# Routing of a mixture-of-experts layer: two experts chosen by eight-largest and replace steps, GpSimd makes half of a split's second parts, a bias row arrives by DMA

## What is computed

```python
mod = jax.nn.silu(c) @ w_ada[l] + b_ada[l]             # 6 x 1024 numbers
sh1, sc1, ga1, sh2, sc2, ga2 = jnp.split(mod, N_MOD, axis=-1)
... # attention and convolution branches, x = x + ga1 * (merged @ w_o)
h2 = modulate(rms_norm(x, g_norm2[l]), sh2, sc2)
# hierarchical_moe: 4 groups of 8 experts
g_logits = xt @ w_rg + b_rg;  g_prob = softmax(g_logits);  g_idx = argmax(g_logits)
g_w = g_prob[g_idx]
e_logits = (xt @ w_re + b_re)[the 8 of group g_idx]
e_val, e_loc = lax.top_k(e_logits, 2)
e_w = softmax(e_val) * g_w                              # weights of the two experts
# each chosen expert: silu(x w1) * (x w3) @ w2 on the tokens that chose it; x = x + ga2 * sum
```

## Time and profile before

| what | us |
|---|---|
| median of 3 runs | 1148.68 |
| range of the runs | 1147.99 to 1148.87 |
| profiled execution, own time | 1147.94 |
| its span, first to last instruction | 1146.1 |
| PE busy in the span | 1116.1 (97%) |
| DVE / ACT / POOL busy | 483.6 / 414.6 / 184.3 |

### The profile page before, as it was taken

The page is one execution under the profiler, slowest core; times in us unless marked ns, Lnnn a source line. Parts: engine busy times, 40 slices in busy tenths (PEclk is TensorE's granted clock), DMA queues, the critical chain, the costliest instruction groups (busy, mean ns, idle before and its releaser), DMA issues.

```text
span 1146.1 us, 15442 instructions
## 1 busy us (share of the span) xinstructions
PE 1116.1 (97%) x5860; PEld 752.1 (66%) x5860; DVE 483.6 (42%) x966; ACT 414.6 (36%) x616; POOL 184.3 (16%) x79
## 2 busy tenths in 40 slices
PE   5899999999999999999999998999999999999998
PEld 3689777874444444444444445978878888888876
DVE  4686344662222222222222214789574653233136
ACT  4543553331111111111111115675464454444234
POOL 0303233000000000000000002100314064342522
PEclk9999999999999999999999999999999999999999
DMA  9968668789999999999999996452434366455451
GB/s 354 381 223 296 215 245 313 285 347 418 421 424 423 422 422 424 423 424 423 423 422 423 424 423 254 148 200 99 143 121 160 124 207 207 150 180 211 158 183 37
DMA packets 96830, 331.75 MB, mean 289 GB/s; under 512 B 8529, under 2 KB 31298, under 8 KB 71170
## 3 DMA queue, kind: packets, MB, share of 16 engines
q1 hardware_dynamic: 96496, 330.58, 74.4%
q0 software_dynamic: 80, 0.26, 0.1%
q10 hardware_dynamic: 194, 0.06, 0.0%
HBM read 329.84 MB, written 1.05 MB: 289 GB/s over the span
## 4 chain that ended last, share of the span: by engine, by line
PE 89%; DMA 4%; DVE 3%; ACT 2%; SPq 2%; issue 1%; DVEq 0%; ACTq 0%
PE ps L1273 19%; PE ps L904 15%; PE ps L905 14%; PE ps L906 14%; PE ps L1313 9%; DMA ring<-in_w_in 4%; PE ps L1250 3%; PE ps L1251 2%; PE ps L1328 1%; PE ps L979 1%; SPq L773 1%; PE ps L1329 1%; DVE ring_r L2110 1%; PE ps L1436 1%; ACT ring_r L1648 1%
## 5 line engine op out<-in xcount | busy, mean ns | idle before, releaser
L866 POOL TENSOR_TENSOR ring_r<-ring,ring_r 128x1024 fp32r<-128x1024 f32 x66 | 172.0, 2627 | 840.4 <-ACT ring_r L1648 840.3
L905 PE MATMUL ps<-ring_r,hl_r 128*128 128x512 f32 x528 | 209.1, 396 | 0.0
L904 PE MATMUL ps<-ring_r,hl_r 128*128 128x512 f32 x480 | 195.2, 407 | 5.6 <-DVE hr_r L2202 4.3
L906 PE MATMUL ps<-ring_r,hr_r 128*128 128x512 f32 x480 | 190.2, 396 | 0.0
L1648 ACT ACTIVATE ring_r<-ring 128x2048 fp32r<-128x2048 f32 x88 | 163.6, 1908 | 59.0 <-PE ps L906 44.7
L2110 DVE TENSOR_TENSOR ring_r<-ring,ring_r 128x2048 fp32r<-128x2048 f32 x55 | 129.6, 2367 | 81.6 <-ACT ring_r L1648 81.3
L1273 PE MATMUL ps<-ring,arena 128*64 128x512 f32 x688 | 153.3, 594 | 0.7 <-DMA ring<-in_w 0.7
L905 PEld LDWEIGHTS ps<-ring_r,hl_r 128*128 128x128 f32 x528 | 99.6, 189 | 21.6
L904 PEld LDWEIGHTS ps<-ring_r,hl_r 128*128 128x128 f32 x480 | 90.5, 188 | 32.1 <-issue 6.3
L1273 PEld LDWEIGHTS ps<-ring,arena 128*64 128x64 f32 x688 | 48.4, 137 | 92.7 <-issue 89.7
L906 PEld LDWEIGHTS ps<-ring_r,hr_r 128*128 128x128 f32 x480 | 90.4, 188 | 21.9
(11 more groups left out here) (381 smaller groups left out, 1820.1 us busy)
## 6 DMA issues: line engine op xcount, KB each, us to landing
ring<-in_w SPq DMA_DIRECT2D x64, 2048.0 KB, 23.1
ring<-in_w_in SPq DMA_DIRECT2D x20, 2048.0 KB, 10.8
gates<-in_w SPq DMA_DIRECT2D x22, 1024.0 KB, 22.8
ring<-in_w_ada SPq DMA_DIRECT2D x16, 1024.0 KB, 9.5
arena<-in_w SPq DMA_DIRECT2D x11, 1024.0 KB, 19.7
uy<-in_w SPq DMA_DIRECT2D x11, 1024.0 KB, 21.7
ring<-in_w_ffn_gate SPq DMA_DIRECT2D x11, 1024.0 KB, 5.4
ring<-in_w_ffn_up SPq DMA_DIRECT2D x11, 1024.0 KB, 7.9
```

The costliest lines, as they stand in the source:

```text
L866: nc.gpsimd.tensor_tensor(rest[:, a:b], w[:, a:b], lead[:, a:b].bitcast(F32), ALU.subtract).then_inc(sem("w_rest_b"), 1)
L904: mm(o, lhsT=a_lead, rhs=b_lead, start=start, stop=False, skip_group_check=True)
L905: mm(o, lhsT=a_lead, rhs=b_rest, start=False, stop=False, skip_group_check=True)
L906: return mm(o, lhsT=a_rest, rhs=b_lead, start=False, stop=stop, skip_group_check=True)
```

## The change

1. Routing on DVE. The group step stays, but its last operation marks the groups that were not chosen (`is_gt`). One `scalar_tensor_tensor` for each token tile puts these experts' logits to about -1e30. `max` (the eight largest of 32) runs once for each tile, the two largest are copied into an otherwise large list, and `match_replace` puts the matching entries to -3e30. Where the values before and after differ, the expert is chosen. ACT takes the exponential of all 32 differences to the largest instead of one number, and the weights come from one product with the 0/1 mask, one sum and one division.
2. PE: `keep_x` for pieces 0 and 1 before the ranks, for 2 and 3 after them; none is run twice.
3. The rests of x for t = 1 move from DVE to GpSimd, which makes each in two steps: a `tensor_scalar` (permuted read of x times the row factor), then a `tensor_tensor` (minus the lead), each 128x512. DVE keeps t = 0, one step for each h.
4. The bias of rows 4, 5, 10 and 11 is loaded by two DMAs from SP into `acc`, after the load of `g2_0` and a wait for `mod_raw` 2. DVE adds part 0 of `g2` as well, in front of part 1 (ACT's copy goes), and `modulation_row` loses its bias matmuls. Semaphore counts follow. `scale1_ready` and `scale2_ready` become one semaphore.

```diff
@@ semaphores of the small banks
-        for n, group in enumerate(("g2", "g3")):
-            small_released[f"{group}_0"] = sem("acc_copied"), n + 3
-            for m in range(1, 4):
-                small_released[f"{group}_{m}"] = sem("acc_added"), 3 * n + m
+        small_released["g3_0"] = sem("acc_copied"), 3
+        for m in range(4):
+            small_released[f"g2_{m}"] = sem("acc_added"), m + 1
+        for m in range(1, 4):
+            small_released[f"g3_{m}"] = sem("acc_added"), 4 + m
@@ SP
+                if name == "g2_0":
+                    sp_.wait_ge(sem("mod_raw"), 2)
+                    for n, c in enumerate(ADA_ROWS[::2]):
+                        sp_.dma_start(acc[64 - 64 * n:128 - 64 * n:32, 1, :],
+                                      A["b_ada"][0, c * COL:(c + 2) * COL].rearrange("(a n) -> a n", a=2)
+                                      ).then_inc(sem("params_in"), 16)
...
             piece_load(sp_, 8, 1, 0)
-            sp_.wait_ge(sem("xp_rest"), 4)
+            sp_.wait_ge(sem("xp_rest"), 2)
+            sp_.wait_ge(sem("xp_rest_b"), 4)
             sp_.wait_ge(sem("moe_gather0_done"), 1)
@@ GpSimd
+            pool.wait_ge(sem("rs1_ready"), 1)
+            for h in range(2):
+                into = xp_r[1][:, 4 * h:4 * h + 4, :]
+                whole = flat(hr[:, :, :], "p k t -> p (k t)")[:, D + h * COL:D + (h + 1) * COL].rearrange("p (j q) -> p j q", q=P)
+                pool.wait_ge(sem("xp_ready"), 2 * h + 2)
+                nc.gpsimd.tensor_scalar(whole, x[:, 1, h * COL:(h + 1) * COL].rearrange("p (q j) -> p j q", j=4),
+                                        rs[:, 1, 1:2], None, ALU.mult).then_inc(sem("xp_rest_b"), 1)
+                pool.wait_ge(sem("xp_rest_b"), 2 * h + 1)
+                nc.gpsimd.tensor_tensor(into, whole, xp_l[:, 1, 4 * h:4 * h + 4, :].bitcast(F32),
+                                        ALU.subtract).then_inc(sem("xp_rest_b"), 1)
@@ PE, modulation_row
-                    mm(o[:, j * P:(j + 1) * P], lhsT=ident[:, at:at + 1].to_broadcast([P, P]),
-                       rhs=ada_acc("g2")[:, j * P:(j + 1) * P], start=True, stop=False)
-                    last = mm(o[:, j * P:(j + 1) * P], lhsT=ident[0:PARAM_N, r:r + 1].to_broadcast([PARAM_N, P]),
-                              rhs=prow[0:PARAM_N, :], start=False, stop=True)
+                    last = mm(o[:, j * P:(j + 1) * P], lhsT=ident[:, at:at + 1].to_broadcast([P, P]),
+                              rhs=ada_acc("g2")[:, j * P:(j + 1) * P], start=True, stop=True)
@@ PE, routing
-            for n in range(4):
+            for n in range(2):
                 keep_x(n)
...
-            keep_x(2, True)
-            keep_x(3, True)
+            keep_x(2)
+            keep_x(3)
...
-                    pe.wait_ge(sem("xp_rest"), 2 * n + 2)
+                    pe.wait_ge(sem("xp_rest"), n + 1)
+                    pe.wait_ge(sem("xp_rest_b"), 2 * n + 2)
                     gather(n)
@@ ACT
-            af(r1[:, 6, :], r1[:, 5, :], ACT.Exp).then_inc(sem("route_exp_ready"), 1)
+            af(rt[:, 3, :, :], rt[:, 1, :, :], ACT.Exp).then_inc(sem("route_exp_ready"), 1)
@@ DVE
             rest_weights(M["cg"], (1,))
+            modulation_sums("g2", 0)
             modulation_sums("g2", 1)
...
+            link(v.memset(rt[:, 3, :, 0:8], 3.0 * BIG))
             row_factors(1, 1, "rs1_ready")
...
-            first_max(g, GROUPS, r1[:, 0, :], gsel, rt[:, 2, :, 0:GROUPS], r1[:, 1, :])
-            v.tensor_tensor(rt[:, 7, :, 0:GROUPS], g, wide_(r1[:, 0, :], GROUPS), ALU.subtract).then_inc(sem("route_sub_ready"), 1)
-            link(v.tensor_scalar(rt[:, 2, :, 0:GROUPS], gsel, BIG, -BIG, ALU.mult, ALU.add))
-            link(v.tensor_tensor(by_group(rt[:, 3, :, :]), by_group(e), per_group(gsel), ALU.mult))
-            link(v.tensor_tensor(by_group(rt[:, 4, :, :]), by_group(rt[:, 3, :, :]), per_group(rt[:, 2, :, 0:GROUPS]), ALU.add))
-            first_max(rt[:, 4, :, :], EXPERTS, r1[:, 2, :], rt[:, 1, :, :], rt[:, 3, :, :], r1[:, 1, :])
-            link(v.scalar_tensor_tensor(rt[:, 5, :, :], rt[:, 1, :, :], -2.0 * BIG, rt[:, 4, :, :], ALU.mult, ALU.add))
-            first_max(rt[:, 5, :, :], EXPERTS, r1[:, 3, :], rt[:, 2, :, :], rt[:, 3, :, :], r1[:, 1, :])
-            v.tensor_tensor(rt[:, 0, :, :], rt[:, 1, :, :], rt[:, 2, :, :], ALU.add).then_inc(sem("chosen_ready"), 1)
-            v.tensor_tensor(r1[:, 5, :], r1[:, 3, :], r1[:, 2, :], ALU.subtract).then_inc(sem("route_sub_ready"), 1)
...
+            link(v.tensor_reduce(least, order, AX.X, ALU.min))
+            link(v.tensor_tensor(others, order, wide_(least, GROUPS), ALU.is_gt))
+            for t in range(TT):
+                mark(v.scalar_tensor_tensor(by_group(rt[:, 4, t, :]), per_group(others[:, t, :]), -BIG, by_group(e[:, t, :]),
+                                            ALU.mult, ALU.add))
+            settle()
+            for t in range(TT):
+                mark(v.max(rt[:, 6, t, 8:16], rt[:, 4, t, :]))
+            settle()
+            link(v.tensor_copy(rt[:, 3, :, 0:2], rt[:, 6, :, 8:10]))
+            for t in range(TT):
+                mark(v.match_replace(rt[:, 2, t, :], rt[:, 3, t, 0:8], rt[:, 4, t, :], -3.0 * BIG))
+            settle()
+            v.tensor_tensor(rt[:, 0, :, :], rt[:, 4, :, :], rt[:, 2, :, :], ALU.is_gt).then_inc(sem("chosen_ready"), 1)
+            v.tensor_tensor(rt[:, 7, :, 0:GROUPS], g, wide_(best, GROUPS), ALU.subtract).then_inc(sem("route_sub_ready"), 1)
+            v.tensor_tensor(rt[:, 1, :, :], rt[:, 4, :, :], rt[:, 6, :, 8:9].to_broadcast([P, TT, EXPERTS]),
+                            ALU.subtract).then_inc(sem("route_sub_ready"), 1)
...
-            x1_rests(0)
+            x1_rest(0)
...
-            x1_rests(1)
+            x1_rest(1)
...
-            link(v.tensor_scalar(r1[:, 8, :], r1[:, 6, :], 1.0, None, ALU.add))
+            link(v.tensor_tensor(rt[:, 4, :, :], rt[:, 3, :, :], rt[:, 0, :, :], ALU.mult))
+            link(v.tensor_reduce(r1[:, 8, :], rt[:, 4, :, :], AX.X, ALU.add))
```

More of the change, by code:

```diff
@@ L1001, in modulation_columns @@
                 o = small.claim(pe, f"cols_{group}")
-                pe.wait_ge(sem("acc_added"), 6)
+                pe.wait_ge(sem("acc_added"), 7)
                 for j in range(COL // P):
@@ L1199, in _ @@
             pe.wait_ge(sem("route_in"), 96)
-            pe.wait_ge(sem("scale2_ready"), 1)
+            pe.wait_ge(sem("scales_ready"), 3)
             for k in range(KD):
@@ L1219, in _, with keep_x @@
             logits(1)
-            def keep_x(n, again=False):
+            def keep_x(n):
                 t, h = TH[n]
-                into = dense.bank(f"moe{n}") if again else dense.claim(pe, f"moe{n}")
+                into = dense.claim(pe, f"moe{n}")
                 mm(into, lhsT=ident, rhs=x[:, t, h * COL:(h + 1) * COL], start=True, stop=True)
@@ L1695, in modulation_sums @@
                     src = small.ready(act_, f"{group}_0")
-                    small.ready(act_, dict(g2="cols_g1b", g3="cols_g1a")[group])
+                    small.ready(act_, "cols_g1a")
                 af(ada_acc(group), src, ACT.Copy).then_inc(sem("acc_copied"), 1)
@@ L1768, in _ @@
                     modulation_row(ROW_AT[unit])
-                if unit in PAIR_AT and PAIR_AT[unit][1] == 0:
-                    modulation_sums(PAIR_AT[unit][0])
+                if unit in PAIR_AT and PAIR_AT[unit] == ("g3", 0):
+                    modulation_sums("g3")
                 if unit == "gate00":
@@ L2176, in modulation_sums @@
                 src = small.ready(dve, f"{group}_{n}")
-                before_ = 3 * (group == "g3") + n - 1
-                dve.wait_ge(*((sem("acc_added"), before_) if n > 1 else (sem("acc_copied"), 3 + (group == "g3"))))
+                if group == "g2" and n == 0:
+                    dve.wait_ge(sem("params_in"), 16 * (len(PARAM_ROWS) + 1))
+                elif group == "g3" and n == 1:
+                    dve.wait_ge(sem("acc_copied"), 3)
+                else:
+                    dve.wait_ge(sem("acc_added"), 3 * (group == "g3") + n)
                 v.tensor_tensor(ada_acc(group), src, ada_acc(group), ALU.add).then_inc(sem("acc_added"), 1)
@@ L2371, in _, with by_group @@
[L2371 to L2382 removed]
+            def by_group(a):
+                return a.rearrange("p (g n) -> p g n", g=GROUPS)
@@ new lines, in per_group @@
+            def per_group(a):
+                return a.unsqueeze(2).to_broadcast([P, GROUPS, PER_GROUP])
+            g, e = lg[:, :, 0:GROUPS], lg[:, :, GROUPS:]
+            best, least, order, others = r1[:, 0, :], r1[:, 1, :], rt[:, 2, :, 0:GROUPS], rt[:, 1, :, 0:GROUPS]
+            link(v.tensor_reduce(best, g, AX.X, ALU.max))
+            link(v.tensor_tensor(order, g, wide_(best, GROUPS), ALU.is_equal))
+            link(v.scalar_tensor_tensor(order, order, -64.0, index[:, :, 0:GROUPS].to_broadcast([P, TT, GROUPS]), ALU.mult,
+                                        ALU.add))
@@ L2384, in _, with x1_rest @@
```

(8 more changed lines are left out.)

37 lines of the change are left out of this document (8 added, 29 removed).

## The result

The changed kernel takes **1150.17 us** (median of 12 runs, 1148.18 to 1153.54) against 1148.70 for the kernel before (12 runs, 1147.78 to 1150.42) on the same chip. The ratio is 1.0017, 95% interval 1.001 to 1.0025: 1.1 to 2.9 us slower, where 1147.4 had been forecast and 1143.4 to 1150.0 as the range.

What follows compares the result with a forecast made beforehand. PE was taken to bound 60 to 240 us and full transfers 260 to 690, with the end hanging on the first `up`. -1.8 (bias) + 0 (`g2`) + 0.5 (routing): 1148.68 - 1.3 = 1147.4 us, range 1143.4 to 1150.0.

Steps and rivals of the forecast that it cites:

- the last sentence of the first part: Start of the first expert `up`: moving it up to about 5 us earlier, or any later, moves the end equally.
- Bias matmuls: Modulation rows on PE: dropping half the matmuls saves 0.91 us each in rows 4 and 5, -1.8 us in all.
- Part 0 of `g2`: DVE's added sum before PE's `tk1` transposes: taken as 0, bound +1.25 us if PE has to wait.
- Selection: DVE's routing from 239.87 us: fewer operations bring `chosen_ready` at 242.4 instead of 244.73, -2.3 us.
- Rival (e): `max` and `match_replace` in the routing are slow: at 1 us each, some 3.3 us later, 1150.7; chance 0.06.
- One rest fewer on DVE, and GpSimd: Routing: one rest less saves DVE 1.1 us, but GpSimd's 4.4 us fall into DVE's path; routing in all +0.5.
- The permuted pass: GpSimd's permuted `tensor_scalar` of x in the routing: taken as 1.0 us, 0.55 for a copy plus 0.45.
- one after the other: Routing: DVE and GpSimd operations alternate without running side by side, putting `gather(0)` at about 249.3 against 248.68.
- rival c: TensorE's clock falls at the gathers after some 3 us standing still, losing 1.7 us: 1149.1; chance 0.10.
- The sum: Whole kernel: -1.8 + 0 + 0.5 on 1147.94 gives 1146.6 profiled, median 1147.4 us.
- rival (a): No lock worth the name on small routing operations: routing gives 3.4 us, 1143.5; chance 0.28 for it or much of it.
- the lock: Routing: DVE and GpSimd exclude each other for a whole instruction; without it the sum would be 3.9 us better.

Runs made afterwards that it cites:

- the repeat: The changed kernel run again with no edit: 1150.24 us, ratio 1.0012; its profiled execution took 1149.02.
- the first execution: The first profiled execution of the changed kernel, the slowest of its twelve: 1153.54 us.
- bias_pad: bias_only with 128 never-executed waits in the untaken branch, moving the exit's jump target to where the kernel before has it: 1146.84 us, ratio 0.9983.
- select_only: The kernel before with the new selection alone; rests, copies of x and bias matmuls as before: 1148.94 us, ratio 0.9999.
- select_keep_pad: The kernel before with the new selection, two copies of x moved behind the ranks, and 16 never-executed waits: 1147.09 us, ratio 0.9983.
- dve_rests_pad: dve_rests with 144 never-executed waits, moving the exit's jump target to where the kernel before has it: 1144.51 us, ratio 0.9967.
- after_pad: The changed kernel with 138 never-executed waits, moving the exit's jump target to where the kernel before has it: 1145.46 us, ratio 0.9973.
- pool_contig_pad: after_pad with GpSimd reading x in order instead of permuted (wrong results, timing only): 1144.66 us, ratio 0.9968.
- edge: The changed kernel with 12 never-executed waits (6 instructions), putting the exit's jump target at a block's start: 1147.54 us, ratio 0.9993.
- dve_rests: The changed kernel with all four rests of x on DVE as before, no GpSimd: 1148.41 us, ratio 0.9998.
- bias_only: The kernel before with only the bias rows loaded by DMA and part 0 of g2 on DVE: 1149.68 us, ratio 1.0012.
- before_pad: The kernel before with 374 never-executed waits, putting the exit's jump target 6 instructions ahead of a block's end: 1153.56 us, ratio 1.0042.
- fill: The changed kernel with two more copies of x on TensorE ahead of gather(0): 1146.18 us, ratio 0.9976.

## Why the prediction was wrong

**The step that failed** is the last sentence of the first part: "Whatever moves that start by up to about 5 us earlier, or by any amount later, moves the end by as much." For the stream it held: block 9 moved by -2.43 in the repeat and the first lead behind the experts by -2.47. But the end of the stage is the later of two chains, and TensorE's own had only a little slack against the stream. The profile of before showed an "issue" gap of 1.69 us at the loop's exit; I left it out, since nothing in the change touches it. The change touches it by being shorter. In place of the 2.4 us gained the runs showed a second wait of 5.01 to 5.31 us for code and some 10 us at half clock behind it, and the copies of x 1.93 us later than before.

**Bias matmuls** (-1.8): right. Sixteen records of line 1011 take 275 ns each, and rows 4 and 5 take 0.89 us each. In the first execution the offset to before falls from 2.2 us ahead of them to 0.4 behind. bias_pad against before is -2.0 us. That the DMAs cost nothing also holds.

**Part 0 of `g2`** (0, bound 1.25): right. ACT starts its lead without a copy ahead, DVE adds part 0 at 84.54 for 0.68, and `tk1`'s transposes (a group from 85.37 on) have no gap ahead:

```profile
84.54 0.68 DVE L2199 TENSOR_TENSOR acc<-ps,acc 128x512 f32<-128x512 f32 x1
...
85.37 1.04 PE L1040 MATMUL ps<-cst,arena 128*128 128x128 f32 x8
```

**Selection** (-2.3): right. Two `MAX8` take 0.29 together, each `MATCH_REPLACE8` 0.18; from the start of the group step (240.26 in the first execution) to the comparison's place (242.57 and 0.2) are 2.5 us, against 4.86. Rival (e) is out. By itself it brings nothing (select_only); with two copies of x moved behind the ranks it brings 1.7 us in the profile (select_keep_pad).

**One rest fewer on DVE, and GpSimd** (together +0.5 with the selection): too dear by 1.3. In the repeat `gather(0)` starts 2.32 us earlier than before, of which 1.5 are there when the routing begins (bias 1.8, less 0.3 from the start): the routing gives -0.8. Without GpSimd (dve_rests_pad) `gather(0)` is 3.42 earlier, at 245.26, and 1.0 to 1.1 of it is there at the beginning: -2.4, which is the forecast's 3.4 less the 1.1 for the rest. So GpSimd costs 1.6 us net, where I had 2.8 (3.9 less 1.1). Two errors stand against each other. The permuted pass takes 2.05 us, not 1.0; in order it still takes 1.57, so the copy was a poor measure for it (its row is on 64 partitions, besides, which I overlooked). But it doesn't hold DVE up for its whole record, as my count "one after the other" had it. after_pad and dve_rests_pad, which enter the routing within 0.05 us of each other:

```profile
240.78 2.05 POOL L889 TENSOR_SCALAR hr<-x,rs 128x512 f32<-128x512 f32 x1 [49.65 <-ACT ya_r L1809]
241.14 0.89 DVE L2395 TENSOR_TENSOR arena<-arena 128x64 f32<-128x64 f32 x1
242.17 1.14 DVE L2403 SCALAR_TENSOR_TENSOR acc_r<-x,rs,ya_r 128x512 fp32r<-128x512 f32 x1
243.75 0.69 DVE L2416 TENSOR_SCALAR hr<-arena 128x64 f32<-128x64 f32 x1
244.47 1.98 DVE L2423 TENSOR_SCALAR arena_r<-cst,hr 128x64 fp32r<-128x64 f32 x4
```

```profile
241.10 0.23 DVE L2383 TENSOR_TENSOR arena<-arena 128x64 f32<-128x64 f32 x1
242.50 1.15 DVE L2392 SCALAR_TENSOR_TENSOR hr_r<-x,rs,ya_r 128x512 fp32r<-128x512 f32 x1
243.81 0.20 DVE L2405 TENSOR_SCALAR hr<-arena 128x64 f32<-128x64 f32 x1
244.04 0.74 DVE L2412 TENSOR_SCALAR arena_r<-cst,hr 128x64 fp32r<-128x64 f32 x4
```

The comparison is held up 0.66 us, the rank step 0.49, the one-hot matrices 1.24 and the flag 0.30 (0.47 instead of 0.17): 2.7 us, less the 1.14 for the rest that GpSimd took over, 1.55. The two `gather(0)` stand 1.56 apart (246.82 and 245.26) and the two spans 1.5 us; the medians differ by 0.95, with intervals that overlap. But the comparison ends at 242.03, 0.8 us before GpSimd's record does, and a rest of 1.14 us runs at full speed beside the record's last 0.66 us. The Trainium skill ("SBUF — State Buffer", section "Who interferes with whom") calls it an exclusive lock. It states the block for a whole instruction for a VectorE instruction in a two-port mode; of one with two SBUF inputs, such as the comparison and the rest, it says that it contends with a GpSimd instruction that reads SBUF. The prediction took the whole instruction for both. The traces agree that the two contend (0.89 instead of 0.23 us); by the records the time held is shorter than the instruction, though spans on POOL are rough.

**The clock** (rival c, 0.10): it fell at the gathers in the first execution, as the rival had it, and in none of seven others with a gap ahead of `gather(0)` (the repeat and after_pad with as long a one, pool_contig_pad, edge, dve_rests_pad, dve_rests and bias_only with 1.14 to 0.57 us). It is a matter of chance and not the cause. Where it fell it was dearer than the rival had it: block 9 is issued 10.64 us behind `gather(0)` there and 7.46 in the repeat, 3.2 us instead of 1.7. The fall from 36 to 42 us belongs to neither kernel: eight of the fourteen profiles have one (0.66 to 0.82), before_pad among them, which executes what before does. The 10 us at half rate behind the exit go with the long wait for code: all five profiles with that wait have them. Of the nine others four have 3.4 us at half rate there (0.93 from 588 to 612 us: fill, edge, bias_pad, dve_rests_pad) and five none, and all nine reach the copies of x in the same 446.1 to 446.5 us.

**The sum.** With the code in its old place the change is worth 1145.46 against 1148.87, -3.4 us: -1.8 for the bias and -0.8 for the routing, and 0.8 that lies within what this measurement can't tell. In the profiles this 0.8 can be placed: before takes 443.73 us from the copies of x to the end, after_pad 442.95. It is the clock fall behind the 2.34 us wait ahead of the copies (0.72 from 700 to 706 us before, 1.00 in after_pad), which pool_contig_pad has too (443.89), so it is no part of the change. The forecast's -1.3 would have been 2.1 us too small by itself, since it charged GpSimd too much, though well inside its range. The time without the code's effect lies in the range of rival (a), but not by its cause: the lock is there and is shorter than I had it. The sign came from the +4.8 us of the code's place.

**Open.** The changed kernel's runs form two groups, 1148.2 to 1149.0 and 1151.5 to 1153.3 us (six each in the repeat's series); after_pad's eleven don't (1145.0 to 1146.6, one at 1148.2). In the repeat's series the mean granted clock over the whole execution is 0.989 to 0.992 in the upper group, and 0.995 in five of the lower six (0.992 in one). The first profiled execution (1153.54), as long as the longest of them, has the two more clock falls shown above, so falls of the clock are the likely difference; where they lie in the others was not traced. Open too is why the second block of code comes 5.8 us after the first although its packet takes 1.1: the weight stream fills the queues at that time (DMA share 1.01), but no run tried it with empty ones.

## What to carry to other kernels

A change of instruction counts on an engine moves all the code behind it. Where that engine takes a jump while the DMA queues are full, look at the first instructions behind it for idle time put down to "issue", and see how far the target is from a block's edge; padding in a branch that isn't taken moves it for nothing. When a change of two lines wins four microseconds, as fill did, check its explanation with one that moves the code alone, before believing it. The best version here is dve_rests_pad, the change without GpSimd's part and with the code where it was: 1144.51 us, 0.9967 of before (0.9955 to 0.9979).

## What the runs showed of the hardware that was not expected

- Behind a taken jump, with the DMA share at 1.01, TensorE waited 1.4 to 1.7 us for the block of the target, and if the target was 1, 6 or 9 instructions ahead of a 256-instruction edge, 5.0 to 5.6 us more (7.30 in all at a distance of 1). At 0, 2 and 63 past the edge there was no second wait. Its work went on 1.5 us after the end of the first packet and 1.2 to 1.4 us after the end of the second.
- Of eight profiles in which TensorE stood still 2.3 us ahead of the copies of x at about 700 us, the granted clock fell behind it in five (0.72 to 0.79 over 6 us) and not in three; the rest of the execution took 443.7 to 444.0 us where it fell, and 442.9 in two of the three where it didn't.
- GpSimd's `tensor_scalar` of 128x512 fp32 takes 2.05 us with a permuted read and 1.57 in order; its copy of twice as many columns, on 64 partitions, takes 1.04. Its `tensor_tensor` of the same size takes 1.27.
- `MAX8` over 32 columns and the copy and `MATCH_REPLACE8` around it are as cheap as any small DVE operation: 0.29 us for two, 0.17 and 0.18.
